# Last two output tiles of the deep projections: four half-width accumulations per pair of tiles, or seven products over half the depth

## The reference

```python
for i in range(DEPTH):                      # two layers
    ...
    x = x + swiglu(rms_norm(x, norm_ffn[i]), ffn_w_in[i], ffn_w_out[i])
...
for i in range(DEPTH_2):                    # four layers
    mod = c_act @ ada_w[i] + ada_b[i]       # six vectors of 1024: 48 columns of 128
    sh1, sc1, g1, sh2, sc2, g2 = jnp.split(mod, 6, axis=-1)
    h = modulate(rmsnorm(x, mix_norm_g[i]), sh1, sc1)
    ...
    x = x + (1.0 + g1)[:, None, :] * y
    h = modulate(rmsnorm(x, ffn_norm_g[i]), sh2, sc2)
    x = x + (1.0 + g2)[:, None, :] * conv_ffn(h, ff_w_up[i], ff_conv_w[i], ff_conv_b[i], ff_w_down[i])
return rmsnorm(x, final_g)
```

## Time and profile before

| | |
|---|---|
| time, median of 3 runs | 2300.94 us (2300.71 to 2301.97) |
| profiled execution: its time | 2300.7 us |
| its span, first to last instruction | 2298.7 us |
| granted TensorE clock over the span | 0.998 |
| PE busy | 2268.2 us (99%), 18014 instructions |
| DVE busy | 1730.2 us (75%) |
| ACT busy | 548.3 us (24%) |
| POOL busy | 184.0 us (8%) |
| DMA | 474.26 MB, mean 206 GB/s |

### The profile page before, as it was taken

The page is one execution under the profiler, slowest core; times in us unless marked ns, Lnnn a source line. Parts: engine busy times, 40 slices in busy tenths (PEclk is TensorE's granted clock), DMA queues, the critical chain, the costliest instruction groups (busy, mean ns, idle before and its releaser), DMA issues.

```text
span 2298.7 us, 45516 instructions
## 1 busy us (share of the span) xinstructions
PE 2268.2 (99%) x18014; PEld 2038.0 (89%) x18014; DVE 1730.2 (75%) x3683; ACT 548.3 (24%) x1388; POOL 184.0 (8%) x296
## 2 busy tenths in 40 slices
PE   8999999999999999999999999999999999999999
PEld 4478999656799997999999799998799998999998
DVE  5866997478579876769986589968769976667883
ACT  2232110027221102213211432212432212213220
POOL 0000011000001010011100011000012100001100
PEclk9999999999999999999999999999999999999999
DMA  6434777751557766468966288674469874456752
GB/s 244 158 129 161 257 276 256 275 186 47 177 202 275 258 257 220 161 218 242 270 234 233 111 233 263 214 262 139 138 202 288 280 260 163 146 173 180 209 179 77
DMA packets 136448, 474.26 MB, mean 206 GB/s; under 512 B 15296, under 2 KB 17472, under 8 KB 135872
## 3 DMA queue, kind: packets, MB, share of 16 engines
q1 hardware_dynamic: 95136, 338.80, 42.2%
q0 software_dynamic: 41120, 132.73, 19.1%
HBM read 470.42 MB, written 1.05 MB: 205 GB/s over the span
## 4 chain that ended last, share of the span: by engine, by line
PE 93%; DVE 5%; ACT 1%; issue 1%; DMA 0%; DVEq 0%; ACTq 0%
PE pair L688 53%; PE bank L688 38%; PE bank L1170 1%; ACT h L1689 1%; PE bank L1000 0%; DVE arena L2955 0%; DVE arena L2995 0%; DVE arena L2991 0%; DVE arena L2363 0%; DVE rstd L2163 0%; DVE arena L3366 0%; PE bank L1111 0%; DVE arena L2438 0%; DMA x<-x_in_dram 0%; DVE h L2172 0%
## 5 line engine op out<-in xcount | busy, mean ns | idle before, releaser
L688 PE MATMUL pair<-arena,ring 128*128 128x128 f32 (+1 forms) x2840 | 389.6, 294 | 3.8 <-issue 2.0
L688 PEld LDWEIGHTS pair<-arena,ring 128*128 128x128 f32 x2840 | 363.6, 192 | 20.0 <-issue 3.6
L688 PE MATMUL bank<-arena 128*128 128x128 f32 (+4 forms) x3172 | 367.0, 278 | 1.9 <-DVE arena L2591 0.8
L688 PEld LDWEIGHTS bank<-arena 128*128 128x128 f32 (+3 forms) x3172 | 348.0, 185 | 16.1 <-issue 6.7
L688 PE MATMUL pair<-arena 128*128 128x128 f32 (+5 forms) x3706 | 340.2, 264 | 2.5 <-DVE arena L2310 1.0
L688 PEld LDWEIGHTS pair<-arena 128*128 128x128 f32 (+4 forms) x3706 | 312.3, 170 | 31.5 <-issue 19.6
L688 PE MATMUL bank<-arena,ring 128*128 128x128 f32 (+1 forms) x2548 | 308.0, 277 | 0.5 <-DVE arena L2363 0.3
L688 PEld LDWEIGHTS bank<-arena,ring 128*128 128x128 f32 x2548 | 295.9, 192 | 3.0 <-DVE arena L2363 0.7
L688 PE MATMUL pair<-h,ring 128*128 128x128 f32 (+1 forms) x2048 | 294.2, 299 | 1.5 <-ACT h L1689 0.9
L688 PEld LDWEIGHTS pair<-h,ring 128*128 128x128 f32 x2048 | 269.9, 192 | 14.6 <-ACT h L1689 1.9
L2758 DVE CUSTOM_DVE_ANT_0 adat<-adat,crow,cols 128x1024 f32<-128x1024 f32 x192 | 243.1, 1277 | 48.0 <-DMA adat<-adaw_dram 48.0
(11 more groups left out here) (320 smaller groups left out, 2460.0 us busy)
## 6 DMA issues: line engine op xcount, KB each, us to landing
ring<-stream_dram SPq DMA_DIRECT2D x638, 512.0 KB, 5.0
adat<-adaw_dram POOLq DMA_DIRECT2D x192, 512.0 KB, 5.3
ring<-stream_dram POOLq DMA_DIRECT2D x80, 256.0 KB, 6.7
arena<-gmrows_dram POOLq DMA_DIRECT2D x1, 2560.0 KB, 11.2
arena<-gmrows_dram POOLq DMA_DIRECT2D x5, 512.0 KB, 9.1
arena<-cmpw_dram POOLq DMA_DIRECT2D x1, 2112.0 KB, 8.6
x<-x_in_dram SPq DMA_DIRECT2D x2, 512.0 KB, 4.5
arena<-mem_in_dram SPq DMA_DIRECT2D x1, 1024.0 KB, 8.8
```

The source lines that it names most:

```text
L688: return nc.tensor.matmul(out, lhsT, rhs, start=start, stop=stop)
```

## The change

The tail becomes seven products too. With A and B the last two output tiles and 1 and 2 the token halves, PE now makes, in this order: product 0 and product 1 into banks 0 and 1, products 2 and 3 into the two banks of the second pair, product 4 into bank 2, and, after these five, products 5 and 6 into the banks of the third pair. Products 0 and 4 add up to B's first half. A's first half is complete with products 0 to 3. Products 5 and 6 complete the second halves. The tail's tiles stand as (N-1, N-2), and in the stream's order of a pair.

DVE's `down_weights` is now called in the third pair too, for the tail. Instead of combining the results in a buffer and then adding, DVE adds each partial result to `x` where it belongs (`early_tail`, and `late_tail`, which stands inside `normalise` at k = 1 and k = 5). ACT copies product 0, and its squares of the second half move into the loop that shifts `h`, at k = 3 and k = 5. The second half's `norm_sum` goes from k = 3 to k = 4 of the next linear, where that is a growing one.

```diff
@@ plan
-                lin.units.append(("tail", tuple(range(lin.N - TAIL, lin.N))))
+                lin.units.append(("tail", (lin.N - 1, lin.N - 2)))
...
@@ semaphore values for the weight sums
-        DOWN_GROUP = [lin.g0 + p + 1 for lin in PLAN.values() if lin.kind == "S" and not lin.grows
-                      for p in range(len(lin.pairs))]
+        DOWN_READ, n_read = [], 0
+        for lin in PLAN.values():
+            if lin.kind == "S" and not lin.grows:
+                for p in range(len(lin.pairs)):
+                    DOWN_READ.append([("down_read", n_read + r + 1) for r in range(3)] + [("mm_done", lin.g0 + p + 1)])
+                    n_read += 3
+                DOWN_READ.append([("mm_done", lin.g0 + lin.groups)] * 4)
...
@@ PE
+                    product(0, lambda j: tile(t + j), lambda j: moving(2 * j)[:, HALVES[0]], t
+                            ).then_inc(sem("half_done"), 1)
+                    pe.wait_ge(sem("down_summed"), 4 * (lin.pair0 + len(lin.pairs)) + 4)
+                    pe.wait_ge(sem("freed_dve"), FREER[g - 2][1])
+                    product(1, lambda j: own[1][:, j, :], lambda j: sums[:, 1, j, :]).then_inc(sem("half_done"), 1)
+                    product(2, lambda j: own[2][:, j, :], lambda j: sums[:, 2, j, :]).then_inc(sem("half_done"), 1)
+                    product(3, lambda j: tile(t + 3 * half_k + j), lambda j: sums[:, 3, j, :]
+                            ).then_inc(sem("half_done"), 1)
+                    product(4, lambda j: tile(t + half_k + j), lambda j: moving(2 * j + 1)[:, HALVES[0]]
+                            ).then_inc(sem("half_done"), 1)
+                    pe.wait_ge(sem("freed_dve"), FREER[g - 1][1])
+                    product(5, lambda j: own[0][:, j, :], lambda j: sums[:, 0, j, :], t + 2 * lin.K,
+                            lambda: norm_sum(norm, 0)).then_inc(sem("mm_done"), 1)
+                    product(6, lambda j: own[3][:, j, :], lambda j: moving(2 * j + 1)[:, HALVES[1]]
+                            ).then_inc(sem("mm_done"), 1)
...
-                late_k = 3 if PLAN[SOURCE[norm]].kind == "S" else 4
+                late_k = 4
...
@@ ACT, squares
+                        if i == 0 and lin.kind == "S" and k in (3, 5):
+                            last_squares(1, (k // 2 - 1,))
-                    if i == 0 and (shift is None or lin.kind == "S"):
+                    if i == 0 and shift is None:
                         last_squares(1)
...
@@ DVE, residual
                     for r in range(4):
-                        if p + 1 < len(lin.pairs):
-                            down_weights(name)
+                        down_weights(name)
                         if between is not None and r < 3:
                             between(3 * p + r)
...
+                def late_tail(k):
+
+                    if k == 1:
+                        dve.wait_ge(sem("mm_done"), lin.tail[1] + 1)
+                        after(max(top, rows))
+                        fifth = banks[tail_places(lin.tail[1])[5]][:, 0:P]
+                        corner.append(chained(plus(B, x[:, B, HALVES[1]], fifth)))
+                        plus(A, x[:, A, HALVES[1]], fifth).then_inc(sem("freed_dve"), 1)
+                    if k == 5:
+                        dve.wait_ge(sem("mm_done"), lin.tail[1] + 2)
+                        after(corner[0])
+                        plus(B, x[:, B, HALVES[1]], banks[tail_places(lin.tail[1])[6]][:, 0:P]).then_inc(sem("freed_dve"), 1)
+                        add_squares(A, HALVES[1], A + TAIL + 1)
...
-                normalise(norm, gain, 0, late_part if lin.kind == "F" else None)
...
+                normalise(norm, gain, 0, late_part if lin.kind == "F" else late_tail)
+                if norm == "final":
+                    gained(0, DK - TAIL)
+                    dve.wait_ge(sem("sq_done"), SQUARES[norm] + DK + TAIL)
+                    gained(DK - TAIL, DK)
```

More of the change, by code:

```diff
@@ L194, in tiles_of @@
         for kind, ns in lin.units:
-            if kind == "pair":
+            if kind in ("pair", "tail"):
                 out += [(2 * j + e, n) for n in ns for e in range(2) for j in range(lin.K // 2)]
@@ L572, in down_own, with tail_places @@
             return gm_out_own(name) if name.startswith("gm_out") else downW[name != "down0"]
+        TAIL_GROUPS = [lin.tail[1] for lin in PLAN.values() if lin.kind == "S" and not lin.grows]
+        def tail_places(g):
+            return [USED[g][0], USED[g + 1][0], *USED[g - 2], LATE[0], *USED[g - 1]]
         FIRST = {}
         for g, place in enumerate(USED):
-            if len(place) > 1:
+            if len(place) > 1 or g in TAIL_GROUPS:
                 FIRST[g] = len(FIRST) + 1
@@ L829, in seven @@
                 t, g = lin.tile0, lin.g0
-                def half(i, base, bank, before):
-                    for k in range(lin.K):
-                        if before is not None and k == 6:
-                            before()
-                        last = mm(bank[:, HALVES[i]], tile(base + k), moving(k)[:, HALVES[i]], k == 0, k == lin.K - 1)
-                        release(last, i == 1 and k < lin.K - 1, base + k)
-                    return last
                 grows = lin.grows
@@ L893, in pair, with tail_pair, product @@
                     ins.then_inc(sem("mm_done"), 1)
+                def tail_pair(t, g):
+                    own = down_own(name)
+                    places = tail_places(g)
+                    def product(n, stationary, move, free=None, before=None):
+                        for j in range(half_k):
+                            if before is not None and j == 5:
+                                before()
+                            ins = mm(banks[places[n]][:, 0:P], stationary(j), move(j), j == 0, j == half_k - 1)
+                            if j == 0 and free is not None:
+                                release(ins, True, free)
+                        return ins
+                    bank_free(g)
+                    bank_free(g + 1)
+                    product(0, lambda j: tile(t + j), lambda j: moving(2 * j)[:, HALVES[0]], t
[13 more added lines that the diff above has]
+                            ).then_inc(sem("mm_done"), 1)
                 p = 0
@@ L916, in seven @@
                     else:
[L917 to L931 removed]
+                        tail_pair(t, g)
                         g += len(ns)
@@ new lines, in plus, with early_tail @@
+                def plus(n, dst, src):
+                    if gate is None:
+                        return V.tensor_tensor(dst, src, dst, ALU.add)
+                    return V.scalar_tensor_tensor(dst, src, gate[:, n:n + 1], dst, ALU.mult, ALU.add)
+                def early_tail():
+                    e = ebuf[:, len(lin.pairs) % 2]
+                    p6, p7, p4, p2 = (banks[b][:, 0:P] for b in tail_places(lin.tail[1])[1:5])
+                    dve.wait_ge(sem("first_copied"), FIRST[lin.tail[1]])
+                    corner = chained(plus(B, x[:, B, HALVES[0]], e[:, 7, :]))
+                    dve.wait_ge(sem("half_done"), HALF[norm] + 2)
+                    second = chained(V.tensor_tensor(e[:, 4, :], p6, e[:, 7, :], ALU.add))
+                    dve.wait_ge(sem("half_done"), HALF[norm] + 3)
+                    after(second)
+                    third = chained(V.tensor_tensor(e[:, 6, :], p7, e[:, 4, :], ALU.add))
+                    top = chained(plus(B, x[:, B, HALVES[1]], e[:, 4, :]))
+                    after(third)
+                    rows = chained(plus(A, x[:, A, :].rearrange("p (i q) -> p i q", i=TT),
+                                        e[:, 6:7, :].broadcast_to([P, TT, P])))
+                    dve.wait_ge(sem("half_done"), HALF[norm] + 4)
+                    after(rows)
+                    plus(A, x[:, A, HALVES[0]], p4).then_inc(sem("x_half"), 1)
+                    add_squares(A - 1, slice(0, TOK), A)
+                    dve.wait_ge(sem("half_done"), HALF[norm] + 5)
+                    after(corner)
+                    plus(B, x[:, B, HALVES[0]], p2).then_inc(sem("x_half"), 1)
+                    return top, rows
@@ new lines, in residual @@
+                if lin.kind == "S":
+                    corner = []
+                    top, rows = early_tail()
+                else:
+                    for n in range(DK - TAIL, DK):
+                        dve.wait_ge(sem("half_done"), HALF[norm] + n - (DK - TAIL) + 1)
+                        add(n, HALVES[0]).then_inc(sem("x_half"), 1)
+                        if n == DK - TAIL:
+                            add_squares(n - 1, slice(0, TOK), n)
+                add_squares(DK - TAIL, HALVES[0], DK - TAIL + 1)
```

67 lines of the change are left out of this document (24 added, 43 removed).

## The result

The changed kernel takes 2324.86 us (median of 4 runs, 2323.26 to 2326.79), the kernel before 2301.45 us (4 runs): a ratio of 1.0101, 95% interval 1.0084 to 1.0119, or 23.4 us slower. The forecast was 2313.4, range 2301 to 2321. The sign and the places were right, the size was not: the time lies 3.9 us above the range. The profiled execution was the slowest of the four, 2326.79 us (span 2325.0, granted clock 0.993 against 0.998). Further on, one run of the kernel before (8293.89 us) and one of the last experiment (7603.92 us) were slow ones; they count in the medians, which they move by less than 0.1 us, and not in the ratios.

The account below looks back on a forecast made before the run. PE's matmul queue was taken as the bound. Products saved -18.3, waits for DVE's sums +22.0 and +0.3, clock +6.0, second half's norm +1.7, program end +0.8: +12.5 us, giving 2313.4 us, range 2301 to 2321.

Parts of the forecast that it names:

- What bounds the kernel: Whole kernel: PE's matmul queue bounds it; time is saved only where that queue shortens, and each added wait costs fully.
- what it removes: PE's tails: seven products instead of eight, 2.46 us less at K = 22 and 1.79 at K = 16, -18.3 us.
- DVE's queue as the gate: Five tails: DVE's sums and ada tiles take 12.3 us, so PE waits at least 2.7 us after its first product.
- The fourth ada tile's landing: Third pair of five linears: its DMA lands 5.3 us after issue, making PE's wait 4.4 us each, +22.0 in all.
- The clock: After each of the five waits the granted clock falls to half, costing 1.2 us each, +6.0; bounds 0 and 8.5.
- The first half's norm: Behind the tail's fifth product PE has 5.4 us left, and the norm fits with 1 us to spare: no cost.
- The second half's norm: Next linear's start: the later norm sum costs 0.45 us before three growing linears, 0.3 before `mla_q`; together +1.7.
- the end of the program: In `cdown3`, two scalings of `h` and both gains stand in DVE's queue behind the last addition: +0.8 us.
- the first (the clock stays up): Rival: the five waits are there but the clock does not fall; sum +6.5, 2307.4 us; chance 0.20.
- the second (a landing as in the quiet stretch): Rival: fourth ada tile lands in 3.4 us, PE waits 2.7 each; 2298.9 us, or 2304.9 with clock falls; chance 0.20.
- the fourth (no wait): Rival: DVE's queue doesn't hold PE up and the change saves what its form promises; 2285 us; chance 0.02.
- The third: Rival: the ada tile lands after 6.9 us and half-level clock stretches lie outside the waits; +23, 2323.9 us; chance 0.11.

Follow-up runs that it names:

- the last experiment: The first experiment's kernel with the second half's norm sum back at k = 3 and six tiles' final gain ahead of the norm: 2284.3 us, ratio 0.9927.
- third experiment: The changed kernel with the third pair's slabs given back later in five linears, so SP sends five slabs 9.8 us later: 2309.37 us, ratio 1.0033.
- the fifth experiment: The changed kernel with plain 896-column additions in place of the fourth and fifth ada tile, which follow behind the third pair's combination: 2303.16 us, ratio 1.0007.
- the first experiment: The changed kernel with two ada tiles before the tail's first weight sum and three behind the third pair's combination, none between sums: 2284.94 us, ratio 0.9924.
- the experiment with small loads: The changed kernel with DMAs of the fourth and fifth ada tile in five third pairs bringing 4 of 1024 columns: 2318.15 us, ratio 1.0073.

## Why the prediction was wrong in size and right in sign

Point by point, by the steps of the prediction:

- **What bounds the kernel** and **what it removes** (-18.3): right. The groups of 22 matmuls still start 2.46 us apart, and without waits a tail at K = 22 is 2.46 us shorter than before.
- **DVE's queue as the gate**: right in form. The last sum's end releases PE in all five tails. With whole ada tiles and the DMA in time the wait is 2.8 to 3.1 us (third experiment) where 2.7 was the lower bound, with the shorter stand-ins 2.1 to 2.4 (fifth).
- **The fourth ada tile's landing**: the step that failed. I took 5.3 us, the median of all 192 tiles, on the ground that "most of them are in" when the tile is issued 5.2 us after the slabs. In `down0` it was issued 5.2 us after (402.52 against 397.31), and the slabs were not in: another 1.16 MB of them went through before the tile's first packet, and in the third experiment, where they are sent later, 7.2 becomes 4.1. A mean of 6.6 instead of 5.3 makes a wait of 5.9 instead of 4.4: +29.6 for +22.0. Some 0.2 a tail of that is DVE's own: from the fourth tile's start to PE's next matmul it takes 5.6 us in `down0`, as worked out, but 5.9 to 6.0 in the other four. The upper bound, 6.9 and waits of 6.0, was the right reading. Five slabs and the fourth and fifth ada tile, 512 KB each, take 8.7 us even at the 420 GB/s of the earlier trace rows, that is from 397.3 to 406.0 at the earliest. That division would have shown that the time I called quiet is full. It would not have given 6.6, since 406.0 is only 3.5 us after the issue; the delay before the first packet is what it leaves out.
- **The clock**: fallen after each of the five, as forecast, but 2.2 us each instead of 1.2, beyond the bound of 1.7. The bound counted one half-level stretch of 3.4 us a wait, and such a stretch did cost 1.4 to 1.7 wherever it stood alone. Four of the five tails had 6.8 us of it. In all runs a stretch of 6.8 came behind waits of 5.7 to 6.3 us, but also once each behind 3.1 and 4.1, so the longer wait made this error larger as a rule: +11.0 for +6.0.
- **`gm_out0`** 0.2 (0.3 forecast), `gm_out3` and `cdown3` nothing: right. **The first half's norm**: nothing at K = 22, right. At K = 16 it is late, which the prediction didn't work out: the last two products leave 2 x 1.79 + 0.45 = 4.0 us there, and from the fifth product's end to the next linear's first matmul it took 4.2 (2103.06 to 2107.26 behind `gm_out3`). Behind `gm_out0` and `gm_out3` these first matmuls come 0.25 us late and the `norm_sum` among them another 0.1, some 0.7 us in both together. **The second half's norm** 1.4 (1.7) and **the end of the program** 0.6 (0.8), from the last experiment: right.
- **Not foreseen**: 0.9 us in `down0`, where the fourth product of the third pair waits for its sum. The kernel before has one such wait of 1.0 elsewhere.

The sum with what was measured: -18.3 + 29.6 + 11.0 + 0.2 + 0.9 + 1.4 + 0.6 = +25.4. The spans of the two profiled executions differ by 26.3, but the kernel before was 1.5 us behind at 35 us (the rows are with the fifth experiment), so the change cost 27.8 in these two. Of the missing 2.4, 0.8 are in the five tails, which from their start to the next linear's start take 41.4 us more than in the first experiment and not 40.6 (the idle times shown leave out 0.2 a tail), and some 0.7 are the first half's norm at K = 16. The last 0.9 stay open.

Of the rivals, the first (the clock stays up), the second (a landing as in the quiet stretch) and the fourth (no wait) fell. The third, at 2323.9 with a chance of 0.11, was the case: a landing near 6.9 and half-level stretches outside the waits. It also lay outside the range, which ended at 2321. Its row was no further from this case than the median was: it is the one row read of a tile with a sum between and the stream beside it.

The Trainium skill's rule on queues ("DMA: Bandwidth & Descriptors", "Queues, rings and completion order": each DMA engine takes turns between its queues packet by packet) gave an estimate of 4.7 us for the landing. The landing was 6.6 on the mean, and 4.5 to 5.3 for a tile of 2 KB. The turns themselves are in the trace of the kernel before, where the fourth tile was issued at 399.45: from 403.0 to 408.4 the two queues moved about the same,

```profile
q1 hardware_dynamic: 313, 1.14, 52.0%
q0 software_dynamic: 284, 1.06, 48.9%
```

but from 399.45 to 403.0 only q1 moved, 310 packets. What the estimate lacked is this start, 2.7 to 3.6 us from issue to first packet beside slabs and 1.2 to 1.3 without them. Why the start is late no run shows.

Its description of a clock that falls in the waits between stretches of matmuls ("TensorE: Matmul & The Clock Gate", "HAM oscillation") is borne out for waits of 3.9 us and more, ten of ten in the change and in the experiment with small loads; for waits of 2.8 to 3.1 us four of five, for waits of 2.1 to 2.4 us two of five.

## What to carry to other kernels

A product that needs sums from another engine saves PE time only if the other engine can deliver inside the work PE has left, so the first number to work out is where that engine's queue stands at that moment; moving three ada tiles behind the sums turned 23 us of loss into 16 of gain. For the landing of a DMA take rows with the same company, not the median of a program. Adding up the bytes in flight and dividing tells whether a stretch is quiet, and gives a lower bound only. Compare two executions from a point where their common part ends, for their starts alone can differ by 3 us. And price an idle stretch of PE with what comes after it, here 11.0 us of slow matmuls on 29.6 us of wait.

## What the runs showed of the hardware

- **The clock falls after short waits too, and not always.** By the tails' waits: up to 1.5 us no fall in eight tails; 1.76 none, 1.98 one; 2.1 to 2.4 two of five; 2.8 to 3.1 four of five; 3.9 to 6.3 ten of ten. A fall cost 1.4 to 1.7 us of longer matmul groups where the lower level held for 3.4 us and 2.0 to 3.0 where it held for 6.8, so equal waits have unequal prices.
- **A small DMA is not a fast one.** Issued some 5 us after five slabs of 512 KB, 2 KB took 4.5 to 5.3 us to their reader and 512 KB took 6.2 to 7.2; with the slabs sent later the 512 KB took at most 3.6 to 4.1.
- **Much of the landing time is gone before the first packet.** Beside the slabs an ada tile's first packet came 2.7 to 3.4 us after its issue in the change, and only then did it get its share; with the slabs sent later it came after 1.2 to 1.3.
- **The same first 35 us take unequal time.** The same operation of DVE started at 33.4 to 33.5 us in three of the nine profiled executions, at 35.1 to 35.3 in four and at 36.5 in two.
